# Weights laid out by the host as contiguous blocks in order of use, and the small inputs packed into three loads

## The chip, the cores and the metric

The kernel runs on one core of one Trainium2 chip. The core has TensorE (PE in the rows, with its weight loads shown apart as PEld), VectorE (DVE), ScalarE (ACT), GpSimd (POOL) and SyncE (SP), which work side by side and wait for each other through semaphores. Transfers between HBM and the on-chip memory are issued by SP and ACT here, each on a queue of its own, and carried out by 16 DMA engines. The metric is the time of one execution on the device, in microseconds (us), as the median of several runs.

## What is computed

The reference is a two-layer transformer block on 256 tokens of width 1024, all in float32:

```python
def reference(x, positions, attn_norm, w_in, ...):
    h = x
    for layer in range(DEPTH):
        h = h + hybrid_mixer(rms_norm(h, attn_norm[layer]), positions, ...)
        hn = rms_norm(h, ffn_norm[layer])
        j = layer // 2
        if layer % 2 == 0:
            h = h + swiglu(hn, dense_w_gate[j], dense_w_up[j], dense_w_down[j])
        else:
            h = h + moe_ffn(hn, moe_router[j], moe_w_gate[j], moe_w_up[j], moe_w_down[j])
    return rms_norm(h, final_norm)

def swiglu(h, wg, wu, wd):
    return (jax.nn.silu(h @ wg) * (h @ wu)) @ wd
```

There are two layers (DEPTH = 2), and a `swiglu` goes from width 1024 to 3584 and back. `hybrid_mixer` multiplies the normed tokens by `w_in` (1024 x 2152), makes three kinds of attention of the result (top-k selected, differential, latent) with rotary embedding of the positions, and multiplies by `w_out` (1024 x 1024). `moe_ffn` routes every token to 2 of 8 experts, each a `swiglu` with its own weights. The small inputs are the norm gains, the positions, the rotary frequencies and four lambda vectors of the differential attention.

## The kernel before

All engines run hand-written programs in a fixed order. The tokens are two tiles (t = 0, 1) of 128 rows. Weights come through `ring`, three slots of 128 partitions x 4096 floats (2 MB each). SP is the only engine that fills them: it walks through the weights in the order of use, waits until the slot is free (`freed`, `chunk_split`: the count `lo_done` of parts that DVE has split) and issues one DMA. In a slot, partition p holds rows p, p+128, p+256, ... of the weight matrix, so before the change a 1024 x 512 block of a wider matrix is read as 8 runs of 2 KB for each partition, a block of a down projection as 4 runs of 4 KB.

Each slot is used in four parts. ACT rounds a part to `w_hi` (`split_hi`, L1074), DVE computes the remainder `w_lo` (`split_lo`, L1372), and PE multiplies by three products, w_hi by hi, w_lo by hi and w_hi by lo (`product`, L761). The two split buffers have room for seven parts (PARTS), so ACT and DVE run ahead of PE by at most seven.

The program starts with the loads. SP issues two of `x` (L522), then the first weight slots. `PROJ` names five column blocks of `w_in` in the order in which they are used, PC (416 columns), PI (512), PK (328), PA (384), PB (512); then follow `UP` (the two weights of the latent attention) and two halves of `w_out`. Before PI's load SP waits for the small loads:

```python
if (layer, c) == (0, "PI"):
    sp.wait_ge(loaded_small, 16 * 6)
```

ACT issues the small ones: positions, the first norm gain (512 KB, one row to all partitions), the rotary frequencies, four lambdas, and three gains of the layer (`load_layer_gains`, L1084 to L1086). After that ACT loads its function table, and squares the tokens of tile 0 and 1 (L1094, step N1). DVE turns the sums into means (L1351), POOL takes the root (L637), DVE writes the normed tokens (L1364, step N2; it waits for the gain), PE transposes them against the identity (L737, step X), ACT and DVE split the transposed tokens into `hnT_hi` and `hnT_lo`. Then ACT reaches PC's first part and waits for slot 0. After the first product (PC, tile 0) DVE computes the rotary angles (`angles`, L1389 on, which waits for `loaded_small`), and ACT their sine and cosine (L1149) and the exponentials of the lambdas (L1152).

Layer 0's dense feed-forward (7 chunks of gate, up, down) takes 21 slots, and the experts take 21 slots each, 168 in all. Two loops of DMAs on SP fill these, the latter with an index computed in a register.

Of the kernel before, what the change touches and what calls it, by code (L numbers as in the profile page):

```python
# [31 lines left out]
WBANKS = 4  # L32

# [48 lines left out]
def hybrid_block(nc, a, out):  # L82
# [10 lines left out]
    x, positions = a["x"], a["positions"]  # L93
    S, D = x.shape[1], x.shape[2]
    DEPTH, _, NIN = a["w_in"].shape
# [9 lines left out]
    CQ, CKV = a["w_uq"].shape[1], a["w_ukv"].shape[1]  # L105
    NF = DR // 2
    FF = a["dense_w_gate"].shape[2]
    NCH = FF // 512
    E = a["moe_w_gate"].shape[1]
# [7 lines left out]
    assert end == NIN  # L117
    PROJ = {"PC": (c_q, end), "PI": (q_i, k_i), "PK": (k_i, k_b), "PA": (q_a, q_i), "PB": (k_b, c_q)}

# [50 lines left out]
    with ctx:  # L170
# [26 lines left out]
        freq = sb("freq", [P, NF])  # L197
        cos = sb("cos", [P, T, NF])
        sin = sb("sin", [P, T, NF])
        cgain = sb("cgain", [P, CQ + CKV])  # L200
        sgain = sb("sgain", [P, 2 * DB])
# [40 lines left out]
        qcT = carve(HC * S).rearrange("p (k s) -> p k s", k=HC)  # L242
# [4 lines left out]
        lamv = qcT[:, 0, :].rearrange("p (l v d) -> p l v d", l=DEPTH, v=4)  # L247
        lamp = qcT[:, 1, 0:DEPTH * 2 * DB].rearrange("p (l v d) -> p l v d", l=DEPTH, v=2)
        lams = qcT[:, 2, 0:2 * DEPTH].rearrange("p (l v) -> p l v", l=DEPTH)
        lame = qcT[:, 2, 64:64 + 2 * DEPTH].rearrange("p (l v) -> p l v", l=DEPTH)  # L250
        pos_i = qcT[:, 3, 0:T].bitcast(I32)
# [10 lines left out]
        router = carve(KT * E).rearrange("p (k e) -> p k e", k=KT)  # L262
# [38 lines left out]
        loaded_ukv = sem("loaded_ukv")  # L301
# [202 lines left out]
        def _(sp):  # L504
            wg, wu, wd = a["moe_w_gate"], a["moe_w_up"], a["moe_w_down"]

            def column_chunk(w, c0, c1):

                return w[:, c0:c1].rearrange("(k p) n -> p k n", p=P)

            def load(use, view, src, rounds=0):
                sp.dma_start(view, src).then_inc(slot_full[use % RING], 16)
# [5 lines left out]
            def wide(use, n, k=KT):  # L518
                return slot(use)[:, 0:k * n].rearrange("p (k n) -> p k n", k=k)

            for t in range(T):
                sp.dma_start(h[:, t, :], x[0, t * P:(t + 1) * P, :]).then_inc(loaded_x[t], 16)  # L522
            for layer in range(DEPTH):
                for c, (c0, c1) in PROJ.items():
                    use = USE[(layer, c)]
                    freed(use - RING)
                    if (layer, c) == (0, "PI"):
                        sp.wait_ge(loaded_small, 16 * 6)
                    load(use, wide(use, c1 - c0), column_chunk(a["w_in"][layer], c0, c1))
                use = USE[(layer, "UP")]  # L530
                freed(use - RING)
                nq, nkv = HC * DC, HC * (DN + DV)
                sp.dma_start(slot(use)[:, 0:2 * nq].rearrange("p (k n) -> p k n", k=2),
                             a["w_uq"][layer].rearrange("(k p) n -> p k n", p=P)) \
                    .then_inc(slot_full[use % RING], 16)
                sp.dma_start(slot(use)[:, 2 * nq:2 * nq + nkv], a["w_ukv"][layer]) \
                    .then_inc(loaded_ukv, 16)
                for half in range(2):
                    use = USE[(layer, f"WO{half}")]
                    freed(use - RING)  # L540
                    load(use, wide(use, 512), column_chunk(a["w_out"][layer], 512 * half, 512 * half + 512))
                if layer == 0:
                    for j in range(NCH + 1):
                        for kind, w in (("g", a["dense_w_gate"][0]), ("u", a["dense_w_up"][0])):
                            if j < NCH:
                                use = USE[("dense", kind, j)]
                                freed(use - RING)
                                load(use, wide(use, 512), column_chunk(w, 512 * j, 512 * j + 512))
                        if j:
                            use = USE[("dense", "d", j - 1)]  # L550
                            freed(use - RING)
                            load(use, wide(use, D, 4),
                                 a["dense_w_down"][0][512 * (j - 1):512 * j, :]
                                 .rearrange("(k p) n -> p k n", p=P))
# [3 lines left out]
            def chunk_at(e, k):  # L558

                e, k = e + k // PER_EXPERT, k % PER_EXPERT  # L560
                j, kind = k // 3 + 1, k % 3
                if kind == 2:
                    return e, j - 1, 2
                return (e, j, kind) if j < NCH else (e + 1, 0, kind)

            def load_chunk(use, e, j, kind):
                w = (wg, wu, wd)[kind]
                w = w[0, e] if isinstance(e, int) else w[0][bass.ds(e, 1)].rearrange("a k n -> (a k) n")
                if kind < 2:
                    load(use, wide(use, 512), column_chunk(w, 512 * j, 512 * j + 512))  # L570
                else:
                    load(use, wide(use, D, 4),
                         w[512 * j:512 * j + 512, :].rearrange("(k p) n -> p k n", p=P))
# [5 lines left out]
            def expert_weights(half):  # L579
                first = MOE_USE + half * E * PER_EXPERT  # L580

                for i in range(RING + 2):
                    if i >= RING:
                        chunk_split(half, i - RING)
                    elif half == 0:
                        freed(first + i - RING)
                    load_chunk(first + i, *((0, 0, i) if i < 2 else chunk_at(0, i - 2)))
                with sp.Fori(0, E - 1) as e:
                    for k in range(PER_EXPERT):
                        chunk_split(half, e * PER_EXPERT + (2 + k))  # L590
                        load_chunk(first + 2 + k + RING, *chunk_at(e, k + RING))

                last = (E - 1) * PER_EXPERT
                for k in range(last + RING, last + PER_EXPERT - 2):
                    chunk_split(half, 2 + k - RING)
                    load_chunk(first + 2 + k, *((E - 1, NCH - 1, 2) if k % PER_EXPERT == 3 * NCH - 3
                                                else chunk_at(0, k)))
# [125 lines left out]
        def _(pe):  # L723
# [102 lines left out]
            def attention(layer):  # L826
                for item in ORDER[layer]:
# [27 lines left out]
                    elif name == "KV":  # L855
                        _, t, i = item
                        b, at = begin(key), 2 * HC * DC + 512 * i
                        pe.wait_ge(loaded_ukv, 16 * (layer + 1))
# [185 lines left out]
            for t in range(T):  # L1044
# [6 lines left out]
                product(b, E, [hnT[:, k, tile(t)] for k in range(KT)], [router[:, k, :] for k in range(KT)]) \  # L1051
# [20 lines left out]
        def _(act):  # L1072
# [3 lines left out]
            def row(v, n):  # L1076

                return v.rearrange("(a n) -> a n", a=1).to_broadcast([P, n])

            def load_gain(v):  # L1080
                act.dma_start(gain[:, :], row(v, D)).then_inc(loaded_gain, 16)
# [35 lines left out]
            with nc.allow_non_contiguous_dma(reason="the positions, one to a partition"):  # L1117
                act.dma_start(pos_i, positions.rearrange("a (t p) -> p (a t)", p=P)).then_inc(loaded_small, 16)
            load_gain(a["attn_norm"][0])
            act.dma_start(freq[:, :], row(a["rope_freq"], NF)).then_inc(loaded_small, 16)  # L1120
            for i, name in enumerate(("q1", "k1", "q2", "k2")):
                v = a[f"diff_lambda_{name}"]
                act.dma_start(lamv[:, :, i, :], v.unsqueeze(0).to_broadcast([P, DEPTH, DB])).then_inc(loaded_small, 16)
            load_layer_gains(0)

            def attention(layer):
                for item in ORDER[layer]:
# [5 lines left out]
                    elif name in ("X", "OT", "XF"):  # L1133
                        if item[2] == 0 or key in TURNED:
                            turn_evac(key, item)
                        if key == (1, "OT", 1, 1):

                            act.dma_start(router, a["moe_router"][0].rearrange("(k p) e -> p k e", p=P)) \
                                .then_inc(loaded_router, 16)
                    elif name == "PC":  # L1140
# [12 lines left out]
                        if t == T - 1:  # L1153

                            act.wait_ge(normed, norm_count(("attn", layer), t))
                            load_gain(a["ffn_norm"][layer])
# [72 lines left out]
            def dense():  # L1229
# [5 lines left out]
                for j in range(NCH + 1):  # L1235
# [17 lines left out]
                    if j == 0:  # L1253

                        act.wait_ge(normed, norm_count(("ffn", 0), 1))
                        load_gain(a["attn_norm"][1])
# [66 lines left out]
            load_gain(a["final_norm"])  # L1323
# [17 lines left out]
        def _(dve):  # L1341
# [44 lines left out]
            def angles():  # L1386

                dve.wait_ge(loaded_small, 16 * 6)
                link(dve.tensor_copy(pos_f, pos_i))  # L1389
                for t in range(T):  # L1390
                    last = dve.tensor_scalar(ang[:, t, :], freq[:, :], pos_f[:, t:t + 1], None, ALU.mult)
# [74 lines left out]
            def attention(layer):  # L1466
                rounds = []
                for item in ORDER[layer]:
# [25 lines left out]
                    elif name == "C2":  # L1494
# [4 lines left out]
                        dve.wait_ge(loaded_cgain, 48 * (layer + 1))  # L1499
# [5 lines left out]
                        if t == 0:  # L1505

                            link(dve.tensor_scalar(sgain[:, :], sgain[:, :], 1.0 - LAM_INIT[layer], None, ALU.mult))
# [331 lines left out]
```

## Time and profile before

| | us |
|---|---|
| median of 3 runs | 1688.43 |
| lowest and highest | 1688.2, 1690.13 |
| profiled execution: span from first to last instruction | 1686.7 |
| PE busy | 1606.9 (95%) |
| DVE, ACT, POOL busy | 1266.3, 1031.7, 61.8 |

The page has the times of one profiled execution: how long each engine was busy, the span in 40 slices, the queues of the DMA engines, the chain of waits that ended last, and the costliest groups of instructions. A line number is one of the kernel before. In the chain of waits each step was released by the one ahead of it. The granted clock of TensorE is given as a share of full speed: 1.00 is its level of 2.4 GHz, 0.50 that of 1.2 GHz, and a value between is a mean over a stretch that had both.

### The profile page before, as it was taken

The page shows a single profiled execution, that of the slowest core. Times are in us where ns is not written, and L with a number is a line of the kernel's source. Part 1 is how long each engine was busy: PE and PEld are TensorE (multiplying, and loading weights), DVE is VectorE, ACT ScalarE, POOL GpSimd, SP SyncE. Part 2 cuts the span into 40 slices and gives each one's busy share as a digit, 9 for nine tenths or more (in the row PEclk, how much of TensorE's full clock was granted, in tenths as well). Part 3 has the DMA queues.
Part 4 walks back from the last instruction along what each step waited for, and adds up shares of the span by engine and source line. Part 5 has one row for each costly group of instructions (what it writes and reads, how often), then busy time and mean ns, then how long its engine had stood idle before and what let it go on. Part 6 is the DMA issues. An engine that isn't in the chain of part 4 may idle for free.

```text
span 1686.7 us, 20762 instructions
## 1 busy us (share of the span) xinstructions
PE 1606.9 (95%) x7214; PEld 1293.4 (77%) x7214; DVE 1266.3 (75%) x1549; ACT 1031.7 (61%) x1311; POOL 61.8 (4%) x126
## 2 busy tenths in 40 slices
PE   6979999999798988999999999999999999999996
PEld 5857788888685777888788788788788788788784
DVE  4676555555447646899889889889988989889895
ACT  4334344444333335778678678678778778778773
POOL 1400000000031000000000000000000000000000
PEclk9965999999898588999999999999999999999999
DMA  8311265545251025999999999999999999999991
GB/s 268 132 50 50 100 217 200 182 168 190 70 194 51 13 88 202 359 349 356 342 335 362 336 336 363 334 336 363 330 339 359 338 335 363 344 325 370 339 362 76
DMA packets 184456, 431.10 MB, mean 256 GB/s; under 512 B 6352, under 2 KB 13008, under 8 KB 184400
## 3 DMA queue, kind: packets, MB, share of 16 engines
q1 hardware_dynamic: 180272, 427.11, 69.8%
q10 hardware_dynamic: 4128, 3.25, 0.7%
q8 instruction: 33, 0.54, 0.1%
q14 instruction: 23, 0.19, 0.0%
HBM read 429.30 MB, written 1.05 MB: 255 GB/s over the span
## 4 chain that ended last, share of the span: by engine, by line
PE 89%; DVE 5%; ACT 3%; issue 2%; DMA 1%; POOL 0%; POOLq 0%; DVEq 0%; SPq 0%; ACTq 0%
PE pair L761 47%; PE work L761 31%; PE work L737 3%; PE work L980 2%; PE pair L737 2%; PE work L992 2%; PE pair L819 1%; PE work L748 1%; PE work L889 1%; ACT w_hi L1074 1%; ACT arena L1203 1%; DMA ring<-in_w_in 1%; DVE nmax L1459 1%; DVE w_lo L1372 0%; DVE arena L1550 0%
## 5 line engine op out<-in xcount | busy, mean ns | idle before, releaser
L1372 DVE TENSOR_TENSOR w_lo<-ring,w_hi 128x1024 fp32r<-128x1024 f32 (+2 forms) x812 | 968.3, 1215 | 265.9 <-ACT w_hi L1074 260.4
L1074 ACT ACTIVATE w_hi<-ring 128x1024 fp32r<-128x1024 f32 (+2 forms) x812 | 848.7, 1054 | 356.7 <-PE pair L761 199.5
L761 PE MATMUL pair<-w_hi,hnT_hi 128*128 128x512 f32 x1120 | 454.0, 405 | 5.1 <-DVE hnT_lo L1380 3.0
L761 PE MATMUL pair<-w_lo,hnT_hi 128*128 128x512 f32 x1120 | 442.6, 395 | 0.0
L761 PE MATMUL pair<-w_hi,hnT_lo 128*128 128x512 f32 x1120 | 442.6, 395 | 0.0
L761 PEld LDWEIGHTS pair<-w_hi,hnT_hi 128*128 128x128 f32 x1120 | 210.5, 188 | 56.2 <-DVE hnT_lo L1380 3.6
L761 PEld LDWEIGHTS pair<-w_lo,hnT_hi 128*128 128x128 f32 x1120 | 210.6, 188 | 50.5 <-issue 3.3
L761 PEld LDWEIGHTS pair<-w_hi,hnT_lo 128*128 128x128 f32 x1120 | 210.4, 188 | 50.8
L761 PE MATMUL work<-w_hi,hidT_hi 128*128 128x512 f32 x552 | 219.7, 398 | 2.6 <-DVE hidT_lo L1618 1.4
L761 PE MATMUL work<-w_lo,hidT_hi 128*128 128x512 f32 x552 | 218.3, 396 | 0.0
L761 PE MATMUL work<-w_hi,hidT_lo 128*128 128x512 f32 x552 | 218.3, 395 | 0.0
L761 PEld LDWEIGHTS work<-w_hi,hidT_hi 128*128 128x128 f32 x552 | 103.7, 188 | 27.3 <-DVE hidT_lo L1618 1.6
L761 PEld LDWEIGHTS work<-w_hi,hidT_lo 128*128 128x128 f32 x552 | 103.7, 188 | 25.1
L761 PEld LDWEIGHTS work<-w_lo,hidT_hi 128*128 128x128 f32 x552 | 103.8, 188 | 24.4
L761 PE MATMUL work<-w_hi,hnT_hi 128*128 128x512 f32 (+3 forms) x224 | 85.5, 382 | 10.3 <-DVE w_lo L1372 5.9
L761 PE MATMUL work<-w_hi,hnT_lo 128*128 128x512 f32 (+3 forms) x224 | 84.2, 376 | 0.0
L761 PE MATMUL work<-w_lo,hnT_hi 128*128 128x512 f32 (+3 forms) x224 | 84.2, 376 | 0.0
L737 PE MATMUL work<-ident,arena 128*128 128x128 f32 (+1 forms) x268 | 59.1, 369 | 19.4 <-DVE arena L1550 19.4
L819 PE MATMUL pair<-arena 64*128 64x256 f32 (+5 forms) x224 | 69.1, 461 | 0.8 <-ACT arena L1074 0.8
L1203 ACT ACTIVATE arena<-pair,nmax 128x128 f32<-128x128 f32 (+1 forms) x64 | 26.3, 417 | 71.0 <-DVE nmax L1459 70.9
L1074 ACT ACTIVATE arena<-work 128x512 f32<-128x512 f32 (+5 forms) x77 | 34.7, 468 | 53.1 <-PE work L761 44.3
L737 PEld LDWEIGHTS work<-ident,arena 128*128 128x128 f32 (+1 forms) x268 | 42.6, 186 | 30.0 <-issue 27.8
(168 smaller groups left out, 1105.0 us busy)
## 6 DMA issues: line engine op xcount, KB each, us to landing
ring<-in_moe_w_gate SPq DMA_DIRECT2D x56, 2048.0 KB, 8.4
ring<-in_moe_w_up SPq DMA_DIRECT2D x56, 2048.0 KB, 8.2
ring<-in_moe_w_down SPq DMA_DIRECT2D x56, 2048.0 KB, 7.8
ring<-in_dense_w_gate SPq DMA_DIRECT2D x7, 2048.0 KB, 7.8
ring<-in_dense_w_up SPq DMA_DIRECT2D x7, 2048.0 KB, 7.8
ring<-in_dense_w_down SPq DMA_DIRECT2D x7, 2048.0 KB, 7.7
ring<-in_w_in SPq DMA_DIRECT2D x4, 2048.0 KB, 8.2
ring<-in_w_out SPq DMA_DIRECT2D x4, 2048.0 KB, 8.0
```

Of the source, the lines that this page charges most:

```text
L737: last = pe.transpose(b[0:n, i * P:(i + 1) * P], src, ident[:, :])
L748: last = pe.matmul(b[:, 0:n], lhs[k], rhs[k], start=(k == 0), stop=(k == len(rhs) - 1))
L761: mm = pe.matmul(b, lhs[x_part][k + kk], w[w_part][:, kk, :], start=(first and kk == 0 and i == 0), stop=(last and kk == 1 and i == 2))
L819: last = pe.matmul(S2[:, m, 0:nk], q, k, start=True, stop=plain)
L889: last = pe.matmul(b[:, 64 * m:64 * m + 64], pt[:, n % 2, m * (t + 1) + kb, :], v, start=(kb == 0), stop=(kb == t))
L980: last = pe.matmul(x_bank[i][:, k * P:(k + 1) * P], hn[:, t, c:c + P], sel[:, t, :], start=(t == 0), stop=(t == T - 1))
L992: pe.matmul(banks[t][c], gselT[:, t, :], yrow[:, 512 * c:512 * c + 512], start=True, stop=True).then_inc(spread_done[half], 1)
L1074: return act.activation(o, i, ACT.Copy)
L1203: last = act.activation(prob[:, n % 3, m, 0:nk], src, ACT.Exp, bias=nmax[:, n, m:m + 1], accum_out=lsum[:, n, m:m + 1])
L1372: dve.tensor_tensor(lo, raw, hi.bitcast(F32), ALU.subtract).then_inc(lo_done, 1)
L1459: dve.tensor_reduce(nmax[:, n, :], src, AX.X, ALU.max, negate=True).then_inc(max_ready, 1)
```

## The change

The host builds new arrays. Every weight slot is one block of [128, n] with partition p's values side by side, up to 16 KB in one run: `attn_weights` (the five blocks of `w_in` and both halves of `w_out` of a layer, as columns of one array), `up_weights`, `dense_chunks` and `moe_chunks` (one block for each slot, the latter already in the order in which the experts' chunks are used). `norm_gains` holds each norm gain copied to all 128 partitions, `layer_gains` the three gains of a layer side by side for all partitions, and `setup` the lambdas, the frequencies and the positions together. The SBUF tensors that receive them are joined in the same manner (`layer_gains`, and `setup` in place of three separate pieces). The order of use, the ring, its waits for free slots, and all arithmetic stay.

```diff
-            def load(use, view, src, rounds=0):
-                sp.dma_start(view, src).then_inc(slot_full[use % RING], 16)
+            def load(use, src):
+
+                n = src.shape[-1]
+                sp.dma_start(slot(use)[:, 0:n], src).then_inc(slot_full[use % RING], 16)
...
-                for c, (c0, c1) in PROJ.items():
-                    use = USE[(layer, c)]
+                at = 0
+                for c in PROJ:
+                    use, n = USE[(layer, c)], KT * width(c)
                     freed(use - RING)
-                    if (layer, c) == (0, "PI"):
-                        sp.wait_ge(loaded_small, 16 * 6)
-                    load(use, wide(use, c1 - c0), column_chunk(a["w_in"][layer], c0, c1))
+                    load(use, a["attn_weights"][layer, :, at:at + n])
+                    at += n
...
-                sp.dma_start(slot(use)[:, 0:2 * nq].rearrange("p (k n) -> p k n", k=2),
-                             a["w_uq"][layer].rearrange("(k p) n -> p k n", p=P)) \
-                    .then_inc(slot_full[use % RING], 16)
-                sp.dma_start(slot(use)[:, 2 * nq:2 * nq + nkv], a["w_ukv"][layer]) \
-                    .then_inc(loaded_ukv, 16)
+                load(use, a["up_weights"][layer])
...
+                w = a["moe_chunks"]
+                load(use, w[n] if isinstance(n, int) else w[bass.ds(n, 1)].rearrange("a p n -> (a p) n"))
...
-                act.dma_start(cgain[:, 0:CQ], row(a["mla_q_norm"][layer], CQ)).then_inc(loaded_cgain, 16)
-                act.dma_start(cgain[:, CQ:], row(a["mla_kv_norm"][layer], CKV)).then_inc(loaded_cgain, 16)
-                act.dma_start(sgain[:, :], row(a["diff_subln"][layer], 2 * DB)).then_inc(loaded_cgain, 16)
+                act.dma_start(layer_gains[:, :], a["layer_gains"][layer]).then_inc(loaded_cgain, 16)
...
-            with nc.allow_non_contiguous_dma(reason="the positions, one to a partition"):
-                act.dma_start(pos_i, positions.rearrange("a (t p) -> p (a t)", p=P)).then_inc(loaded_small, 16)
-            load_gain(a["attn_norm"][0])
-            act.dma_start(freq[:, :], row(a["rope_freq"], NF)).then_inc(loaded_small, 16)
-            for i, name in enumerate(("q1", "k1", "q2", "k2")):
-                v = a[f"diff_lambda_{name}"]
-                act.dma_start(lamv[:, :, i, :], v.unsqueeze(0).to_broadcast([P, DEPTH, DB])).then_inc(loaded_small, 16)
+            load_gain(("attn", 0))
+            act.dma_start(setup, a["setup"]).then_inc(loaded_small, 16)
             load_layer_gains(0)
```

On ACT the start of the program before, up to the first part of the first weight slot (in square brackets the semaphore that an instruction waits for):

```order
L1118 DMA arena<-in_positions 128x2x1
L1081 DMA gain<-in_attn_norm 128x1024
L1120 DMA freq<-in_rope_freq 128x16
L1123 DMA arena<-in_diff_lambda_q 128x2x32
L1123 DMA arena<-in_diff_lambda_k 128x2x32
L1123 DMA arena<-in_diff_lambda_q 128x2x32
L1123 DMA arena<-in_diff_lambda_k 128x2x32
L1084 DMA cgain<-in_mla_q_norm 128x256
L1085 DMA cgain<-in_mla_kv_norm 128x128
L1086 DMA sgain<-in_diff_subln 128x64
L1094 ACT_TABLE_LOAD
L1094 ACTIVATE hn,stat<-h 128x1024 [waits loaded_x0]
```

The same place on ACT now:

```order
L1049 DMA gain<-in_norm_gains 128x1024
L1084 DMA arena<-in_setup 128x274
L1052 DMA layer_gains<-in_layer_gains 128x448
L1060 ACT_TABLE_LOAD
L1060 ACTIVATE hn,stat<-h 128x1024 [waits loaded_x0]
L1060 ACTIVATE hn,stat<-h 128x1024 [waits loaded_x1]
L1046 ACTIVATE hnT_hi<-work 128x4x128 [waits job_done] x2
L1046 ACTIVATE w_hi<-ring 128x832 [waits slot_full0]
```

Ten DMA issues ahead of the table load have become three, and the gain, which was second behind the positions, is first. What follows on ACT is the same.

On SP the start of the program before, the two loads of x and the first weight slots:

```order
L522 DMA h<-in_x 128x1024 x2
L512 DMA ring<-in_w_in 128x8x416
L512 DMA ring<-in_w_in 128x8x512 [waits loaded_small]
L512 DMA ring<-in_w_in 128x8x328
L512 DMA ring<-in_w_in 128x8x384 [waits lo_done]
```

The same place on SP now:

```order
L518 DMA h<-in_x 128x1024 x2
L511 DMA ring<-in_attn_weights 128x3328
L511 DMA ring<-in_attn_weights 128x4096
L511 DMA ring<-in_attn_weights 128x2624
L511 DMA ring<-in_attn_weights 128x3072 [waits lo_done]
```

The second weight load no longer waits, so five loads go out back to back; every run of 416, 512 or 328 floats has become one of 3328, 4096 or 2624. On PE, DVE and POOL no instruction has moved.

## Rows read from the trace of the kernel before

**Rows 1.** The page: busy time, share of the span, instructions.

```profile
span 1686.7 us, 20762 instructions
PE 1606.9 (95%) x7214; PEld 1293.4 (77%) x7214; DVE 1266.3 (75%) x1549; ACT 1031.7 (61%) x1311; POOL 61.8 (4%) x126
```

**Rows 2.** Stretches: length, each engine's busy us and instructions, granted clock, DMA share, GB/s.

```profile
0.00:5.00 5.00, 0.00 (x0) 0.00 (x0) 0.00 (x0) 0.00 (x0) 1.28 (x12) 1.00 0.44 121
5.00:9.00 4.00, 0.00 (x0) 0.00 (x0) 0.00 (x0) 0.81 (x1) 0.00 (x0) 1.00 1.01 388
9.00:16.00 7.00, 2.77 (x13) 2.70 (x14) 3.60 (x6) 3.98 (x8) 2.10 (x2) 1.00 0.73 206
...
206.00:430.00 224.00, 223.30 (x983) 180.63 (x984) 123.66 (x126) 95.53 (x104) 0.00 (x0) 1.00 0.54 192
652.00:1664.00 1012.00, 1010.30 (x4529) 812.15 (x4530) 888.24 (x843) 768.16 (x814) 0.00 (x0) 1.00 0.93 340
```

**Rows 3.** The chain of waits in order of time, 13 to 30 us: start, length, what.

```profile
1.74 14.13 DMA ring<-in_w_in
...
15.88 0.91 ACT w_hi L1074
...
27.12 0.96 ACT w_hi L1074
```

**Rows 4.** Timeline, rows of ACT and DVE: start, length, what [idle before it].

```profile
0.82 0.47 ACTq L1118 DMA_DIRECT2D arena<-in_positions  x1
...
6.83 1.33 ACTq L1086 DMA_DIRECT2D sgain<-in_diff_subln  x1
8.20 1.28 ACT L1094 ACT_TABLE_LOAD   x1 [8.20 <-issue]
9.49 1.06 ACT L1094 ACTIVATE hn<-h 128x1024 f32<-128x1024 f32 x1
...
10.54 1.04 ACT L1094 ACTIVATE hn<-h 128x1024 f32<-128x1024 f32 x1
...
11.80 1.28 DVE L1364 SCALAR_TENSOR_TENSOR hn<-h,stat,gain 128x1024 f32<-128x1024 f32 x1
...
15.20 0.60 ACT L1074 ACTIVATE hnT_hi<-work 128x512 fp32r<-128x512 f32 x1 [0.26 <-PE work L737]
...
21.77 0.16 DVE L1389 CAST arena<-arena 128x2 f32<-128x2 int32 x1
```

**Rows 5.** DMA issues of the first 3 us: size, us from issue to landing.

```profile
h<-in_x SPq DMA_DIRECT2D x1, 512.0 KB, 4.3
...
h<-in_x SPq DMA_DIRECT2D x1, 512.0 KB, 6.4
gain<-in_attn_norm ACTq DMA_DIRECT2D x1, 512.0 KB, 7.5
```

**Rows 6.** What SP's queue waited for, 0 to 80 us: us in total, times, longest.

```profile
SPq L512 <- DMA arena<-in_diff_lambda_k: 14.1, 1, 14.1
```

**Rows 7.** The page: DMA issues of the experts' weights; then queues with packets and time.

```profile
ring<-in_moe_w_gate SPq DMA_DIRECT2D x56, 2048.0 KB, 8.4
...
ring<-in_moe_w_down SPq DMA_DIRECT2D x56, 2048.0 KB, 7.8
...
q8 instruction: 33, 0.54, 0.1%
```

**Rows 8.** Who waited for whom, 700 to 1600 us, and later rows of the chain.

```profile
ACT w_hi L1074 <- DMA ring<-in_moe_w_down: 1.4, 2, 0.9
...
258.19 11.20 PE pair L761 x48
...
1102.41 5.60 PE pair L761 x24
```

**Rows 9.** Two like stretches of the layers' attention, in the columns of group 2.

```profile
68.58:173.71 105.13, 91.82 (x388) 69.42 (x388) 69.01 (x191) 39.28 (x125) 10.27 (x19) 0.64 0.12 41
504.40:607.35 102.95, 88.97 (x387) 67.61 (x388) 68.92 (x191) 40.53 (x126) 10.26 (x19) 0.67 0.12 42
```

More of the change, by code:

```diff
@@ L540, in _, with load_chunk @@
                     freed(use - RING)
-                    load(use, wide(use, 512), column_chunk(a["w_out"][layer], 512 * half, 512 * half + 512))
+                    load(use, a["attn_weights"][layer, :, at:at + SLOT])
+                    at += SLOT
                 if layer == 0:
[L543 to L573, printed above, removed]
+                    for n in range(PER_EXPERT):
+                        use = USE[("dense", "g", 0)] + n
+                        freed(use - RING)
+                        load(use, a["dense_chunks"][n])
+            ahead = 2
+            def load_chunk(use, n):
+                w = a["moe_chunks"]
+                load(use, w[n] if isinstance(n, int) else w[bass.ds(n, 1)].rearrange("a p n -> (a p) n"))
             def chunk_split(half, n):
@@ L580, in expert_weights @@
                 first = MOE_USE + half * E * PER_EXPERT
[L582 to L584 removed]
+                for n in range(RING + ahead):
+                    if n >= RING:
+                        chunk_split(half, n - RING)
                     elif half == 0:
[L586 to L587 removed]
+                        freed(first + n - RING)
+                    load_chunk(first + n, n)
                 with sp.Fori(0, E - 1) as e:
[L589 to L597, printed above, removed]
+                    for n in range(PER_EXPERT):
+                        chunk_split(half, e * PER_EXPERT + (ahead + n))
+                        load_chunk(first + ahead + n + RING, e * PER_EXPERT + (ahead + n + RING))
+                for n in range((E - 1) * PER_EXPERT + RING + ahead, E * PER_EXPERT):
+                    chunk_split(half, n - RING)
+                    load_chunk(first + n, n)
             expert_weights(0)
@@ L1050, in _ @@
                     emptied(pe, (1, "XF", t, i))
-                product(b, E, [hnT[:, k, tile(t)] for k in range(KT)], [router[:, k, :] for k in range(KT)]) \
+                product(b, E, [hnT[:, k, tile(t)] for k in range(KT)], [router[:, k * E:(k + 1) * E] for k in range(KT)]) \
                     .then_inc(job_done, 1)
@@ L1829, with rows @@
     nc = bacc.Bacc("TRN2", target_bir_lowering=False, num_devices=1)
-    arrays = {n: np.ascontiguousarray(inputs[n]) for n in _INS}
-    arrays["rope_freq"] = (THETA ** (-np.arange(16) / 16.0)).astype(np.float32)
+    f = {n: np.asarray(v) for n, v in inputs.items()}
+    depth, d = f["attn_norm"].shape
+    experts, ff = f["moe_w_gate"].shape[1], f["moe_w_gate"].shape[3]
+    def rows(w):
+        k, n = w.shape
+        return w.reshape(k // P, P, n).transpose(1, 0, 2).reshape(P, (k // P) * n)
@@ new lines, in everywhere, with chunks, attn_weights @@
+    def everywhere(v):
+        return np.broadcast_to(v, (P,) + v.shape)
+    def chunks(gate, up, down):
+        found = []
+        for j in range(ff // 512 + 1):
+            c, last = slice(512 * j, 512 * j + 512), slice(512 * j - 512, 512 * j)
+            if j < ff // 512:
+                found += [rows(gate[:, c]), rows(up[:, c])]
+            if j:
+                found.append(rows(down[last]))
+        return found
+    def attn_weights(layer):
+        w_in, w_out = f["w_in"][layer], f["w_out"][layer]
+        return np.concatenate([rows(w_in[:, c0:c1]) for c0, c1 in PROJ_COLUMNS.values()] +
+                              [rows(w_out[:, 512 * i:512 * i + 512]) for i in range(2)], axis=1)
@@ new lines @@
+    lambdas = np.stack([f[f"diff_lambda_{n}"] for n in ("q1", "k1", "q2", "k2")], axis=1).reshape(-1)
+    freq = (THETA ** (-np.arange(16) / 16.0)).astype(np.float32)
+    places = np.ascontiguousarray(f["positions"].reshape(-1, P).T).astype(np.int32).view(np.float32)
+    moe = np.empty((experts * 3 * (ff // 512), P, SLOT), np.float32)
+    for e in range(experts):
+        for n, w in enumerate(chunks(f["moe_w_gate"][0, e], f["moe_w_up"][0, e], f["moe_w_down"][0, e])):
+            early = e and n < 2
+            late = e < experts - 1 and n == 3 * (ff // 512) - 1
+            moe[e * 3 * (ff // 512) + n + (2 if late else -1 if early else 0)] = w
@@ new lines @@
+    arrays = {
+        "x": f["x"],
+        "setup": np.concatenate([everywhere(lambdas), everywhere(freq), places], axis=1),
+        "norm_gains": np.stack([everywhere(v) for v in (
+            f["attn_norm"][0], f["ffn_norm"][0], f["attn_norm"][1], f["ffn_norm"][1], f["final_norm"])]),
+        "layer_gains": np.stack([everywhere(np.concatenate([f[n][layer] for n in (
+            "mla_q_norm", "mla_kv_norm", "diff_subln")])) for layer in range(depth)]),
+        "attn_weights": np.stack([attn_weights(layer) for layer in range(depth)]),
+        "up_weights": np.stack([np.concatenate([rows(f["w_uq"][layer]), rows(f["w_ukv"][layer])], axis=1)
+                                for layer in range(depth)]),
+        "dense_chunks": np.stack(chunks(f["dense_w_gate"][0], f["dense_w_up"][0], f["dense_w_down"][0])),
+        "moe_chunks": moe,
+        "router": rows(f["moe_router"][0]),
+    }
```

72 lines of the change are left out of this document (32 added, 40 removed).

## The prediction, made before the change was run

> **What bounds the kernel now.** I read the page's busy times first, then the table of stretches, then the chain of waits at the places where TensorE stands idle, then who waited for a DMA, and last the DMA issues.
>
> TensorE is busy for 95% of the span [rows 1]. The table of stretches shows where the other 5% is [rows 2]: in the dense stage (206 to 430 us) and in the experts (652 to 1664 us) it is idle for 0.7 and 1.7 us, at a granted clock of 1.00. These two stages are 1236 of 1686.7 us, and a transfer can shorten them only by waking TensorE sooner, for which there is no idle time left. Nor does TensorE's own pace depend on the transfers: 48 products take 11.20 us where the DMA engines are busy for 0.54 of the time, and 24 take 5.60 us where they are busy for 0.93 [rows 2, 8]. Both are 0.233 us a product. So nine tenths of the bytes whose layout changes belong to stages where the layout is not what ends last.
>
> The one place where the chain goes through a transfer is the start [rows 3]. The chain begins with the first weight load (issued at 1.74 us, landed 14.13 us later), which is followed at 15.88 us by ACT's first split, and that by the first product. Beside it, and nearly as long, runs a second path that the chain doesn't name: ACT issues ten small loads from 0.82 to 8.16 us, loads its table, squares the two token tiles from 9.49 us, and ends the last transposed half at 15.80 us [rows 4]. The weights landed at 15.87 us. Both paths must become shorter, or nothing is gained.
>
> **ACT's ten issues become three.** The first starts at 0.82, the last ends at 6.83 + 1.33 = 8.16 us [rows 4], so ten took 7.34 us. The one for the positions took 0.47 us, the last 1.33. With three of some 0.5 us the table load starts at about 2.3 us, not 8.20, and ends at 3.6. It doesn't wait for x; the squares do. Tile 0 landed at 0.81 + 4.3 = 5.1 us, tile 1 at 1.27 + 6.4 = 7.7 (issues start at 0.81 and 1.27, [rows 5] has the times to landing). So of the 5.9 us saved on ACT's sequencer, at most 9.49 - 5.1 = 4.4 can be passed on: from there the landing of x is late next.
>
> Tile 1's square needs 1.06 us after tile 0's. If x lands as before, the second square starts at 7.7 us in place of 10.54, which is 2.8 us earlier; if tile 1 is in by 6.15, it is 4.4 earlier. I expect tile 1 earlier than before, since between its packets and those of tile 0 now stands the gain (128 runs of 4 KB) and not the 256 runs of 4 bytes of the positions: the 16 engines were busy for 0.44 of the first 5 us and moved 121 GB/s, and from 5 to 9 us, with x and the gain in them, 388 GB/s [rows 2]. Two tiles and the gain are 1.57 MB; at 388 GB/s, with the first byte at 1.8 us (I allow one us from the issue), that is 5.8 us, and with 0.8 allowed from the last packet to the semaphore a landing at about 6.6. Tile 1's square is then 10.54 - 6.6 = 3.9 us earlier. The gain landed at 1.33 + 7.5 = 8.8 us [rows 5]; it must be there when DVE starts to norm at 11.80 - 3.9 = 7.9 us, and being issued first it is expected by 6. All behind it (means, root, norm, transposes, two splits) is computing that doesn't change, so ACT is ready for the weights at 15.80 - 3.9 = 11.9 us. Bounds: 2.8 and 4.4 us earlier.
>
> The Trainium skill says on its page "DMA: Bandwidth & Descriptors", section "Issuing engines are not separate DMA queues", that issuing from several engines only saves the sequencer's issue time, and that this time is usually small beside the transfer. By that rule alone ACT's removed issues would be worth little, and the time would stay at 1688. The rows differ: ten issues held ACT for 7.34 us, longer than either tile of x took to land.
>
> **The first weight load.** What must have passed before it lands: x 1.05 MB, gain 0.52, PC's block 1.70, setup 128 x 274 x 4 bytes = 0.14, layer gains 128 x 448 x 4 = 0.23, together 3.64 MB. That is no less than before (121 x 5 + 388 x 4 + 206 x 7 GB/s x us = 3.6 MB until 16 us, [rows 2]). What goes is the small runs: from 9 to 16 us the engines were busy for 0.73 and moved only 206 GB/s, against 388 at a share of 1.01 with runs of 4 KB [rows 2]. At 388 GB/s from 1.8 us, 3.64 MB take until 11.2 us; with some 0.7 us to the landing it is 11.9. If the slow first stretch stays (121 GB/s until 5 us gives 0.6 MB), the rest of 3.04 MB needs 7.8 us and the landing is at 13.5. If the mean of the whole start stays, nothing is gained. I take 12.1, nearer the first, since the stretch from 5 to 9 us is of the very packets that now stand at the start. ACT's first split then starts at 12.1 in place of 15.88: **3.8 us earlier**. Bounds: 2.4 (landing at 13.5) and 4.4.
>
> **SP's removed wait.** SP stood 14.1 us for the last lambda before it issued PI's load [rows 6]. The load now goes out at about 2.2 us, behind PC's on the same queue, and with PK's adds 2.1 + 1.3 MB after 11.9 us: PI lands at about 17, PK at about 21. ACT wants PI at 27.12 - 3.8 = 23.3 us [rows 3]. It was not late before either: there ACT came from its sine and exponential, so this edit is worth 0 by itself, and hidden by PC's product and ACT's tables. What it may cost is dealt with as a rival.
>
> **All that follows the first product** keeps its distances and starts 3.8 us earlier. PA's and PB's loads wait for slots that DVE frees, which is earlier by the same amount.
>
> **The long runs.** A gate slot of 2 KB runs lands in 8.4 us, a down slot of 4 KB runs in 7.8 [rows 7]. So doubling the run is worth 0.6 us; runs of 16 KB perhaps one us in all. In 900 us of the experts ACT waited for a slot of a down block twice, 1.4 us in all [rows 8], and it runs up to seven parts ahead of TensorE, which showed none of it. Worth 0 in the sum. If that cover were gone, these 1.4 us would be what longer runs can give. The one load of UP in place of two, the two issues fewer of the layer's gains and the router's load lie beside TensorE that is busy: 0.
>
> **Sum.** 1686.7 - 3.8 = 1682.9 us for the span of the profiled execution. The median of the runs stands 1.7 us above that span, so 1688.43 - 3.8 = **1684.6 us**. A measurement of this kernel can tell about 0.2%, 3.4 us, from no change; the forecast lies just beyond it.
>
> **Rivals.**
>
> *The bytes, not the runs (chance 12%).* The start moves no fewer bytes. If the rate of 206 GB/s comes from x and weights competing and not from short runs, PC lands at 13.5 to 15.9 and the gain is 0 to 2.4 us: about 1687.2. For it speaks that the first 5 us were slow before many short runs were under way; against it that the engines were idle for a quarter of the time from 9 to 16 us with work queued.
>
> *The small loads are starved (8%).* SP's removed wait kept 3.4 MB away from the small loads. DVE wants `setup` at about 21.77 - 3.8 = 18 us (the angles started at 21.77, [rows 4]). If ACT's packets came after all of SP's, 3.64 + 3.4 MB at 388 GB/s, they would land near 20 us and the angles, the sine and PI's split would be 2 us late: gain 1.8, about 1686.6. It decides nothing as long as setup lands by 18. Were the gain held back too, behind PC, the norm would start at 12 and not at 11.80 [rows 4], and nothing would be won.
> The same page of the Trainium skill ("Queues, rings and completion order") says that a DMA engine takes turns between queues packet by packet; by that rule ACT's 24 packets an engine are through by the time PC is, and this rival falls. No row of before has long packets on one queue against short ones on the other.
>
> *The clock takes some back or adds to it (8%).* The two layers' attention stretches hold the same work: 105.13 us at a mean granted clock of 0.64, and 102.95 us at 0.67 [rows 9]. In the level of 1.2 GHz that is 75.7 and 67.9 us, so 7.8 us more at the lower level cost 2.2 us. A start that is 3.8 us earlier can move where the clock falls; such a move is worth 1 to 3 us, either way: 1682.5 or 1687. The three runs before, 1.9 us apart, hold it already.
>
> *Long packets are slow, and the experts become bound by loads (4%): the slower side.* The only 16 KB packets in this trace are those of instructions: 33 packets took 0.1% of 16 engines' span [rows 7], 0.001 x 16 x 1686.7 / 33 = 0.82 us each. A slot is 128 packets of 16 KB, 8 to an engine: at 0.82 us it is 6.5 us of every engine, while the experts use 168 slots in 1012 us, 6.02 each. Then the loads would end last, and 168 x 0.5 = 90 us would be added: 1775. It decides from 6.02 / 8 = 0.75 us a packet. Against it: from 2 KB to 4 KB runs the landing got shorter, 8.4 to 7.8 us.
>
> *Something beyond the start is won (4%).* If the parts' waits for DMA mattered in the transitions between stages, another 1 to 2 us: 1683.
>
> **How the numbers follow.** My forecast, a gain of 2.4 to 4.4 us around 3.8, has 64%. Within it about three quarters lie beyond the 3.4 us that can be told: 0.49. With half of the clock's case and the last one 0.57, say 0.58, faster by over 0.2%. Slower by over 0.2% is the long packets and a remainder for what I have not thought of, 0.05. The rest, 0.37, is within 0.2%. The range: the forecast's upper end of 4.4 us with a us for the clock and the spread of runs, 1683.0; at the other end the bytes' and the starved loads' cases down to a gain of 0.6, 1687.8. The long packets' case is left out.
>
> **What would show it.** Right: ACT's table load near 2.3 us, its first square near 5, its second near 6.6, its first split near 12.1, the next gap (PI's split after the exponential) at 23.3 with the same length; dense and experts stages as long as before to a us, at the same 5.60 us; a DMA share in the experts that is lower than 0.93. Wrong: a first split that starts well after ACT is free (the bytes), a DVE that waits for setup before the angles (starved), TensorE idle in the experts with a DMA as the releaser (long packets), or a first split 3.8 us earlier and an end that is not (the clock).

## The result

| | us |
|---|---|
| before, median of 20 runs | 1688.97 (1685.58 to 1691.04) |
| after, median of 20 runs | 1693.01 (1690.37 to 1695.37) |
| after to before | 1.0027, 95% interval 1.002 to 1.0033 |
| profiled execution of after: span | 1689.7 (before 1686.7) |

The change made the kernel 4.0 us slower, by an interval of 3.4 to 5.6 us, where 3.8 us less were forecast. The profiled execution agrees: 3.0 us more in the span.

The page of the kernel after, its span, its busy times and its queue of weight loads:

```profile
span 1689.7 us, 20807 instructions
PE 1612.8 (95%) x7214; PEld 1296.5 (77%) x7214; DVE 1266.5 (75%) x1549; ACT 1030.6 (61%) x1311; POOL 61.7 (4%) x126
...
q1 hardware_dynamic: 30096, 427.11, 67.2%
...
ring<-in_moe_chunks SPq DMA_DIRECT2D x168, 2048.0 KB, 9.0
```

TensorE does the same 7214 matrix instructions and is busy for 5.9 us longer than in [rows 1]. VectorE, ScalarE and GpSimd are not. The bytes of the weight queue are the same, in 30096 packets in place of 180272, and a slot of the experts takes 9.0 us to land where it took 8.4 or 7.8 [rows 7].

The start, first as the timeline of ACT, then as the chain of waits (start, length, what):

```profile
1.74 0.45 ACTq L1052 DMA_DIRECT2D layer_gains<-in_layer_gains  x1
2.22 1.28 ACT L1060 ACT_TABLE_LOAD   x1 [2.22 <-issue]
6.11 1.06 ACT L1060 ACTIVATE hn<-h 128x1024 f32<-128x1024 f32 x1 [2.61 <-DMA h<-in_x]
7.88 1.06 ACT L1060 ACTIVATE hn<-h 128x1024 f32<-128x1024 f32 x1 [0.62 <-DMA h<-in_x]
13.05 3.25 ACT L1046 ACTIVATE w_hi<-ring 128x832 fp32r<-128x832 f32 x4
...
15.15 6.48 PE work L733 x24
...
28.33 20.23 PE work L733 x96
```

ACT's first split has moved from 15.88 [rows 3] to 13.05 us. So the start was won, by 2.8 us. What has been lost lies behind it. The stretches, in the columns of [rows 2]:

```profile
0.00:5.00 5.00, 0.00 (x0) 0.00 (x0) 0.00 (x0) 1.28 (x1) 1.28 (x12) 1.00 0.59 201
9.00:16.00 7.00, 4.50 (x19) 4.03 (x20) 6.06 (x8) 4.07 (x7) 1.55 (x1) 1.00 1.00 425
...
652.00:1664.00 1012.00, 1012.00 (x4520) 812.38 (x4519) 888.05 (x841) 766.87 (x813) 0.00 (x0) 1.00 0.90 340
```

In the same 1012 us of the experts TensorE began 4520 instructions, not 4529, at the same granted clock of 1.00 and with no idle time at all. Two pieces of the chain of after, one from the dense stage and one from the experts, show why:

```profile
257.08 11.25 PE pair L733 x48
...
718.12 5.62 PE pair L733 x24
```

48 products take 11.25 us in place of 11.20, and 24 take 5.62 in place of 5.60 [rows 8]: about 1.0 ns more for each. The two stages have 21 x 48 + 168 x 24 = 5040 of them. Counted in the two traces from the same product to the same product, the dense stage is 0.96 us longer and the experts 3.98 us, together 4.9 us. It is the same where the DMA engines are half idle (dense) and where they are busy for 0.90 of the time, so it doesn't look like contention. What else had changed for TensorE? Its instructions are the same, in the same order. But the change removes the tensor `freq` (64 bytes in each partition), and all tensors allocated behind it stand 64 bytes lower. `w_hi`, whose values stream through every one of these products, went from byte 171872 of the partition to 171808; `w_lo` follows it.

### The profile page after: what moved, and what is told of

It reads as the page before. It is cut to its first block, busy times and chain, and to the rows that moved or that the text cites. A ratio compares the mean times of both kernels' runs of the same rounds, so it can differ in the third digit from the quotient of the medians.

```text
span 1689.7 us, 20807 instructions
## 1 busy us (share of the span) xinstructions
PE 1612.8 (95%) x7214; PEld 1296.5 (77%) x7214; DVE 1266.5 (75%) x1549; ACT 1030.6 (61%) x1311; POOL 61.7 (4%) x126
## 3 DMA queue, kind: packets, MB, share of 16 engines
q1 hardware_dynamic: 30096, 427.11, 67.2%
## 4 chain that ended last, share of the span: by engine, by line
PE 89%; DVE 5%; ACT 3%; issue 2%; DMA 0%; POOL 0%; POOLq 0%; DVEq 0%; SPq 0%; ACTq 0%
PE pair L733 47%; PE work L733 31%; PE work L709 3%; PE work L952 2%; PE pair L709 2%; PE work L964 2%; PE pair L791 1%; PE work L720 1%; PE work L861 1%; ACT w_hi L1046 1%; ACT arena L1164 1%; DVE nmax L1420 1%; DVE w_lo L1333 0%; DVE arena L1511 0%; DMA h<-in_x 0%
```

## The experiments

### The same chip, and the 64 bytes

Four kernels ran on one chip, each timed against before. The first two are the kernels before and after, unchanged, so that a property of the kernel can be told from one of the chip. The fourth has 6 runs, the others 12.

> The kernel before, unchanged, on the chip that runs the next three. If TensorE's slower pace after the change (24 products in 5.62 us, not 5.60) belongs to the kernel, this one shows 5.60 us and a time equal to before. If it belongs to the chip that took the profile, this run and the changed kernel show the same pace on the same chip.

> The changed kernel on the same chip. If the slower pace belongs to the kernel: 5.62 us for 24 products and 3 to 5 us slower than before. If it belongs to the chip: the pace of the run before, and then the 2.8 us won before the first product should show at the end, less what the clock takes.

The third gives the removed bytes back, the fourth takes them from the kernel before:

```diff
         mask_k = sb("mask_k", [P, CHUNK], BF16)
+        room = sb("room", [P, 16])
```

> The changed kernel with an unused tensor of 64 bytes a partition where freq stood, so that every tensor behind it, w_hi and w_lo among them, is again at the address it had before. If the shift of w_hi and w_lo by 64 bytes causes the slower pace: 5.60 us for 24 products and about 4.4 us (4700 products x 0.9 ns) less than the changed kernel, near 1688. If the long packets cause it: 5.62 us and the changed kernel's time.

```diff
-        freq = sb("freq", [P, NF])
...
         w_lo = sb("w_lo", [P, PARTS, 1024], F32R)
+        freq = sb("freq", [P, NF])
```

> The kernel before with freq allocated last, so that w_hi and w_lo and all between stand 64 bytes lower, as in the changed kernel; loads and layout as before. If the addresses cause the slower pace: 5.62 us for 24 products and 4.4 us slower than before. If the long packets or the packed loads do: no change from before.

| kernel | w_hi at | median us | to before, 95% interval | span of the profile |
|---|---|---|---|---|
| before | 171872 | 1689.41 | 0.9999 (0.999 to 1.0007) | 1688.3 |
| after | 171808 | 1693.08 | 1.0025 (1.0013 to 1.0037) | 1691.5 |
| after, 64 bytes given back | 171872 | 1687.66 | 0.9987 (0.9977 to 0.9996) | 1685.6 |
| before, `freq` last | 171808 | 1696.97 | 1.0041 (1.0026 to 1.0057) | 1690.9 |

In the chain of waits of each, a piece of 24 products in the experts. Before on this chip:

```profile
714.89 5.60 PE work L761 x24
```

After on this chip:

```profile
714.22 5.62 PE work L733 x24
```

After with the 64 bytes given back:

```profile
712.05 5.60 PE work L734 x24
```

Before with `freq` moved to the end:

```profile
713.84 5.62 PE work L761 x24
```

The pace goes with the address, not with the chip, not with the layout of the weights and not with the packed loads: both kernels are slow at 171808 and fast at 171872. The new loads, with the addresses as they were, make the kernel faster by 0.13% (0.04 to 0.23), which is 2.2 us, and its profile is 2.7 us shorter than that of before on the same chip. That is what the change does as such.

Between the third kernel and after lie 5.4 us, between before and the fourth about 7, both more than the 4.9 us of the pace. Part of the rest goes with the granted clock. Of after's first 20 runs those with a mean granted clock of 0.948 took 1690.37 to 1691.84 us, the three with 0.946 took 1692.01 to 1692.24, those with 0.945 took 1692.98 to 1695.37. One profile of after is of the first kind (0.948) and one, on this chip, of the last (0.945). Between the same two products, near 430 and 652 us, where layer 1's attention lies, they took 221.4 and 224.4 us; from 440 to 470 us the granted clock was 0.89 in the former and 0.77 in the latter. So the 3.0 us are lost there. What decides when the clock rises there stays open, and whether the address has a part in it.

### Which tensor, and which addresses

The 64 bytes stood ahead of all small tensors. The next kernel puts them directly ahead of `w_hi`, so that only `w_hi` and `w_lo` return; two more have 32 and 96 bytes there, in place of 64.

```diff
+        room = sb("room", [P, 16])
         w_hi = sb("w_hi", [P, PARTS, 1024], F32R)
```

> The changed kernel with the 64 unused bytes a partition right ahead of w_hi, so that only w_hi and w_lo return to their old addresses (171872 in place of 171808) and the small tensors between stay moved. If the addresses of w_hi and w_lo are the cause: 48 products in 11.20 us, as before. If one of the small tensors is: 11.25 us.

> The same with 32 bytes: w_hi at 171840, a multiple of 64 bytes. If the pace needs 64-byte alignment it is here at its best, at or under 11.20 us for 48 products; if 96 bytes past a multiple of 128 is what counts, 11.25 us.

> The same with 96 bytes: w_hi at 171904, a multiple of 128 bytes. If alignment to a larger block helps: under 11.20 us for 48 products. If only the one address of the kernel before was good: 11.25 us.

| bytes ahead of w_hi | w_hi at | past a multiple of 128 | 24 products, us | one time, us |
|---|---|---|---|---|
| 0 (after) | 171808 | 32 | 5.62 | 1691.44 |
| 32 | 171840 | 64 | 5.60 | 1686.1 |
| 64 | 171872 | 96 | 5.60 | 1686.95 |
| 96 | 171904 | 0 | 5.44 to 5.49 | 1659.0 |

Returning `w_hi` and `w_lo` alone is enough. The two move together in all these kernels, and the products that stream the one have the same pace as those that stream the other. The 96 bytes, meant as one more point of the table, gave a kernel that is 30 us faster. Its chain of waits in the experts, and the stretch of 700 to 1600 us, in a second profile of the same program:

```profile
708.12 5.44 PE pair L734 x24
...
714.00 5.49 PE pair L734 x24
```

```profile
700.00:1600.00 900.00, 900.00 (x4128) 738.79 (x4127) 805.29 (x772) 692.57 (x741) 0.00 (x0) 1.00 0.93 353
```

In 900 us TensorE began 4128 instructions, where after began 4028, at the same granted clock. So 512 columns cost 227 to 229 ns where `w_hi` starts at a multiple of 128 bytes, 233.3 ns at 64 and 96 bytes past one, and 234.3 at 32 past. Every 512-column block of the two tensors in these two stages is 2048 bytes long, so the start of the tensor decides for all of them. That the address counts is shown; that it counts by multiples of 128 is only the simplest reading of four addresses within 96 bytes, and no second multiple of 128 was tried as a start. Nor does the gain reach shorter products: 48 products of 384 columns in layer 0's attention begin 175.9 ns apart with `w_hi` at 171872 and 175.7 at 171904.

It was timed, and the same address was given to the kernel before (32 bytes ahead of `w_hi` there):

> The changed kernel with w_hi at a multiple of 128 bytes, timed against before. If TensorE's pace of 227 ns a product in the one profile belongs to the address: about 1659 us, ratio near 0.982.

> The kernel before with 32 unused bytes a partition ahead of w_hi, which puts it at the same multiple of 128 bytes (171904); loads and layout as before. If the address alone gives the pace: 227 ns a product and 1660 to 1661 us. If at this pace the short runs of 2 KB no longer keep up (the experts then want 353 GB/s), TensorE waits for slots and it is several us slower than the changed kernel at the same address.

| kernel, w_hi at 171904 | median us | to before, 95% interval |
|---|---|---|
| after's layout | 1658.26 | 0.9816 (0.98 to 0.9833) |
| before's layout | 1660.53 | 0.9824 (0.9808 to 0.984) |

The address is worth 29 us to either kernel. In the profile of before's layout, 28.2 us shorter than that of before, the dense stage is 5.9 us shorter and the experts 20.8 us, counted from the same product to the same product: 26.7 us, or 5.3 ns for each of the 5040 products. The rest lies in the stretches around them. Between the two layouts remain 2.3 us, as much as at the other address, though the intervals overlap. The experts now want 353 GB/s, and both layouts deliver it. Who waited for whom from 700 to 1600 us, with the blocks of the changed kernel:

```profile
ACT w_hi L1047 <- PE pair L734: 88.3, 220, 2.1
ACT w_hi L1047 <- DMA ring<-in_moe_chunks: 29.8, 32, 2.0
```

and with the short runs of before:

```profile
ACT w_hi L1075 <- DMA ring<-in_moe_w_up: 7.9, 8, 1.5
ACT w_hi L1075 <- DMA ring<-in_moe_w_gate: 6.9, 7, 2.0
ACT w_hi L1075 <- DMA ring<-in_moe_w_down: 5.4, 7, 1.4
```

ACT waits for slots for 29.8 us with the blocks and 20.2 us with the short runs, against 8.0 us in after and 2.5 us in before (1.4 on the down blocks [rows 8], 1.1 on the others). TensorE stays busy for 900.00 of 900.00 us in both: the parts split ahead still cover it. The expectation that the short runs would fall behind at this pace did not come true.

### What won the start

Two kernels each do one half of the change, with `w_hi` at its old address. The first packs only the small loads, the second lays out only the weights.

```diff
-            with nc.allow_non_contiguous_dma(reason="the positions, one to a partition"):
-                act.dma_start(pos_i, positions.rearrange("a (t p) -> p (a t)", p=P)).then_inc(loaded_small, 16)
...
+            act.dma_start(setup, a["setup"]).then_inc(loaded_small, 16)
...
                     if (layer, c) == (0, "PI"):
-                        sp.wait_ge(loaded_small, 16 * 6)
+                        sp.wait_ge(loaded_small, 16)
                     load(use, wide(use, c1 - c0), column_chunk(a["w_in"][layer], c0, c1))
```

> The kernel before with only the small loads packed (three issues on ACT); weights as before, w_hi at the old address; SP still waits for setup before PI's load. If the issues and short runs of the small loads were what held the start: ACT's first square near 6 us and its first split near 13, as in the changed kernel. If the weights' long runs are needed: a first split still at 14.5 to 15.9.

```diff
                     if (layer, c) == (0, "PI"):
                         sp.wait_ge(loaded_small, 16 * 6)
-                    load(use, wide(use, c1 - c0), column_chunk(a["w_in"][layer], c0, c1))
+                    load(use, a["attn_weights"][layer, :, at:at + n])
```

> The kernel before with only the weights laid out as blocks; eleven small loads and SP's wait as before, w_hi at the old address. If the small loads hold the start: ACT's first square stays at 9.49 us and its first split at 15.8. If the weights' layout alone is enough: a first split before 15.

The timeline of ACT with only the small loads packed:

```profile
6.21 1.06 ACT L1092 ACTIVATE hn<-h 128x1024 f32<-128x1024 f32 x1 [2.70 <-DMA h<-in_x]
...
13.18 3.25 ACT L1078 ACTIVATE w_hi<-ring 128x832 fp32r<-128x832 f32 x4
```

and with only the weights laid out:

```profile
4.28 0.73 ACTq L1094 DMA_DIRECT2D arena<-in_diff_lambda_k  x1
5.04 4.51 ACTq L1055 DMA_DIRECT2D cgain<-in_mla_q_norm  x1
9.58 0.46 ACTq L1056 DMA_DIRECT2D cgain<-in_mla_kv_norm  x1
...
10.90 1.28 ACT L1065 ACT_TABLE_LOAD   x1 [10.90 <-issue]
12.20 1.06 ACT L1065 ACTIVATE hn<-h 128x1024 f32<-128x1024 f32 x1
```

The packed small loads alone bring the first split to 13.18 us, nearly all of the gain (2.7 of 2.8 us). The weights' layout alone makes the start worse: the first square comes at 12.20 us and not at 9.49 [rows 4], since one issue on ACT, of a load whose neighbours took 0.5 to 0.8 us, took 4.51. On the full change nothing of this is seen, as ACT has no small issue left at that time. One time each was taken, 1685.81 us for the small loads and 1692.21 for the weights, where before had 1690.05 in the median of 7; one time says no more than the order. The traces say the rest: behind the start, the kernel with short weight runs and the one with the full change at the old address take the same time to 0.3 us, once the 1.5 us that the latter's slow first products cost (next section) are taken off. So the 2.2 us of the change are those of the small loads, and nothing here shows a gain from the new layout of 427 MB of weights.

### The clock at the first product

In the profile of after the first 24 products take 6.48 us, in that of before 4.79 us in the same piece of the chain. This looked like a loss by the earlier start, with TensorE at its lower level after being idle. A kernel was made that keeps it busy before:

```diff
             pe.wait_ge(consts_ready, 1)
+            for _ in range(38):
+                pe.transpose(work[3][:, 0:P], ident[:, :], ident[:, :])
```

> The changed kernel with the 64 bytes restored ahead of all small tensors, and 38 more transposes of the identity on TensorE between 2.3 us and the first transposes of the tokens, into a bank that nobody reads before it is overwritten. If TensorE starts PC's product at its lower level because it was idle before: the product of PC, tile 0, takes 4.8 us in place of 6.5 and the whole of the 2.8 us won before it is kept, so 1 to 1.5 us less than the kernel with the 64 bytes alone. If the level rises at a fixed time whatever TensorE does: no change.

Its first piece of the chain:

```profile
14.42 5.38 PE work L734 x24
```

The piece took 5.38 us, neither figure, and the median is 1686.76 us, a ratio of 0.9986 (0.9976 to 0.9996), where the kernel without the transposes had 0.9987. Nothing was won that can be told. The other profiles say why the first reading was wrong. The kernel before, run again on the chip of the four kernels above:

```profile
18.18 6.49 PE work L761 x24
```

and before with `freq` moved, which begins at the same time:

```profile
18.29 4.78 PE work L761 x24
```

The same work at the same time takes 6.49 or 4.78 us. In the former, as its timeline has it, a product of 416 columns begins every 0.35 us until 21.8 and every 0.19 after, though over such slow products the clock's column shows 1.00 (15 to 19 us in after's profile). The changed kernel has both kinds too. In its profile on that chip the products are 0.19 us apart from the start:

```profile
15.44 0.35 PE L733 MATMUL work<-w_lo,hnT_hi 128*128 128x416 f32 x1
15.63 0.35 PE L733 MATMUL work<-w_hi,hnT_lo 128*128 128x416 f32 x1
```

In its first profile they are 0.35 us apart until 18.8 us. So the moment at which TensorE becomes quick differs by over 3 us between executions of one kernel, which changes the length of this piece by 1.7 us. It does so in either kernel and is no part of the change. What sets it was not found.

## Why the prediction was wrong

**The stages bound by TensorE.** The prediction gave them 0: transfers have no idle time to take away there, and the pace of the products doesn't depend on the transfers. Both statements held (with the new layout too the products take 11.20 and 5.60 us, once the address is the old one). The step that failed is "All that follows the first product keeps its distances". It took the pace as a constant of the program, because no instruction of TensorE had moved, and passed over the one edit that touched the operands: a tensor of 64 bytes removed ahead of `w_hi`. That cost 4.9 us by the pace and 5.4 in the medians, and turned 2 us of gain into 4 of loss. The step had a second fault, which no term of the sum covered: the distances also change with the clock, by 1.7 us at the first products and by 3.0 us in layer 1's attention, between executions of one kernel.

**ACT's issues.** The direction was right, the term too large. Three issues ended at 2.2 us and the table load at 3.5, as said. But tile 0 landed at 6.1 us, not 5.1, perhaps as the gain is now issued beside it (no run separates this); and tile 1 at 7.86, not 6.6, where before it was 7.7. The sum took 3.9 us for this path, from an estimate of tile 1's landing that was 1.3 us too early. The bound for a tile 1 that lands as before, 2.8 us, is what came: 10.54 to 7.88 is 2.7, and the first split moved by 2.8.

**The first weight load** was no longer late. It took 10.7 us from issue to landing in place of 14.1, landed at 12.4 us against a forecast of 12.1, and ACT was free only at 13.05. The rival of "the bytes, not the runs" fell, as the start moved no fewer bytes. But the prediction took all small runs together for the cause, and either half of the change is enough: the load took 11.1 us with only the small loads packed and 10.8 us with only the weights laid out. What held the first split back in the latter was ACT's issues. Whether it is the runs or the number of issues that counts in the small loads was not separated. Nor was the 206 GB/s from 9 to 16 us a rate of short runs alone: nothing stood behind that load on SP's queue until 16.3 us, and in the kernel with only the weights laid out it was 180 GB/s.

**SP's removed wait** was worth 0, as said: with the small loads packed and the wait kept, SP stood 6.0 us before it issued PI's load, and the start is the same to 0.1 us. In after PI's load landed at 17.4 us, where 17 was forecast. `setup` landed at 8.5 us and the angles on DVE began at 18.9, 2.8 earlier like all the rest, so the small loads were not starved.

**The long runs** were worth 0 in the sum, as said, but for a wrong reason. I expected them to land up to 1 us sooner; in the experts they land later (9.0 us), and in the dense stage no sooner (7.9 us, where before had 7.8 and 7.7), though the packets' share of the engines' time fell from 69.8% to 67.2%. ACT's waits for slots from 700 to 1600 us grew from 2.5 to 8.0 us, still hidden. The rival of slow long packets was wrong in its price: in the profile 30096 packets took 0.672 x 16 x 1689.7 / 30096 = 0.60 us on average, not 0.82, below the 0.75 from which it would have decided.

**The clock** did take something and give something back in single runs, 1.7 and 3.0 us in the two places named above, as the rival had it.

The slower side got 0.05, and that is the real fault: it was built from mechanisms of the loads alone, and the edit that mattered, a tensor taken away, stood in none of them. With the address left as it was, the forecast of 1684.6 us would have stood against about 1687, of the right sign, with a gain nearly twice too large.

## What to carry to other kernels

A kernel bound by TensorE has a pace, and for the 512-column products of this one that pace depends on where the streamed operand starts in SBUF. The one start tried at a multiple of 128 bytes was the best of four, so try such a start first (order the allocations, or pad), and try others 32 bytes apart before anything else is tuned. When a change adds, removes or resizes any tensor, write out the addresses of the big ones before and after, and read the time of one product in both profiles. And a removed cost at the start is worth only what the next thing in line allows: here ACT was freed 6 us sooner, and the landing of x let 2.8 of them through.

## What the runs showed of the hardware

- At the 2.4 GHz level a product of 512 fp32r columns took 227 to 229 ns with the streamed tensor at byte 171904 of the partition (a multiple of 128), 233.3 ns at 171840 or 171872 (64 or 96 past one), 234.3 ns at 171808 (32 past). Between 171872 and 171904 lie 1.7% of this kernel's time. Products of 384 columns showed no difference (175.9 and 175.7 ns).
- A DMA issue on ACT took 4.51 us where SP's queue held the weight load with runs of 13 KB and ACT's own loads had runs of 128 bytes; with short runs on both queues the longest took 1.33 us. One profile showed it.
- In the experts a weight slot of 2 MB in runs of 16 KB landed in 9.0 us, in runs of 2 KB in 8.4, in runs of 4 KB in 7.8, while the packets' own time fell by 3.6% with the long runs.
- TensorE's products at the start become quick at a moment that differs by over 3 us between executions of one kernel (18.8 us, or before 15.4), which makes 1.7 us of time. The clock's column of the profile shows 1.00 over both.
